# Handing over between two layers in token halves

## The reference, cut to what matters

```python
def _hybrid_layer(x, ..., w_out, g_post):
    ...
    o = jnp.concatenate([o_mla, o_fox], axis=-1) @ w_out
    return x + _rms_norm(o, g_post)

def second_block(x, w_in, ..., norm_g, final_g):
    ...
        h = _rmsnorm(x, norm_g[l])
        proj = h @ w_in[l]
        (qa, kca, vca, ksa, vsa, kwa, vwa, za, ga,
         qb, kb, vb, zb) = jnp.split(proj, offsets, axis=-1)
```

## Time and profile before

| | |
|---|---|
| median of 3 runs | 1853.12 us (1852.43 to 1853.68) |
| the profiled execution | 1853.12 us |
| its span | 1851.4 us |
| mean granted TensorE clock | 0.994 |
| PE busy | 1823.4 us (98%) |
| DVE busy | 1047.4 us (57%) |
| ACT busy | 665.6 us (36%) |
| POOL busy | 36.3 us (2%) |

### The profile page before, as it was taken

One profiled execution on the slowest core, in us unless ns is written; L12 is line 12 of the kernel. 1 busy time (PEld: TensorE's weight loads), 2 busy tenths in 40 slices (PEclk: granted clock), 3 DMA queues, 4 the chain that ended last, 5 costly groups with the idle time before them and its releaser, 6 DMA issues.

```text
span 1851.4 us, 25537 instructions
## 1 busy us (share of the span) xinstructions
PE 1823.4 (98%) x9060; PEld 1514.8 (82%) x9060; DVE 1047.4 (57%) x1768; ACT 665.6 (36%) x1279; POOL 36.3 (2%) x58
## 2 busy tenths in 40 slices
PE   9999999999999999999999999999999999999997
PEld 7788888888888887878868887888888888888887
DVE  7643434444433787853348954766767566665334
ACT  6532332322223544432226342433433333443222
POOL 0000000000000000000002000000000000000001
PEclk9999999999999999999999999999999999999998
DMA  6322222222232333232237363211112222124333
GB/s 237 106 86 91 79 79 91 86 84 82 89 102 80 126 114 113 91 112 93 91 101 218 102 227 124 70 57 57 68 57 69 92 68 79 66 70 136 115 115 102
DMA packets 56021, 186.16 MB, mean 101 GB/s; under 512 B 6688, under 2 KB 11168, under 8 KB 55456
## 3 DMA queue, kind: packets, MB, share of 16 engines
q1 hardware_dynamic: 51328, 170.78, 27.6%
q0 software_dynamic: 4640, 14.68, 3.0%
HBM read 177.05 MB, written 8.39 MB: 100 GB/s over the span
## 4 chain that ended last, share of the span: by engine, by line
PE 90%; DVE 5%; DVEq 2%; ACT 1%; issue 1%; POOL 0%; POOLq 0%; ACTq 0%
PE strip L421 23%; PE strip L423 22%; PE strip L422 22%; PE scores L421 4%; PE scores L422 3%; PE scores L423 3%; PE outputs L423 2%; PE outputs L422 2%; PE outputs L421 1%; PE scores L476 1%; PE scores L869 1%; PE scores L828 1%; PE scores L897 1%; DVE wl L1433 1%; DVEq L1438 0%
## 5 line engine op out<-in xcount | busy, mean ns | idle before, releaser
L421 PE MATMUL strip<-xh,wh 128*128 128x512 f32 (+1 forms) x1976 | 779.7, 395 | 5.7 <-DVE xl L1825 3.2
L423 PE MATMUL strip<-xh,wl 128*128 128x512 f32 (+1 forms) x1976 | 768.0, 389 | 0.0
L422 PE MATMUL strip<-xl,wh 128*128 128x512 f32 (+1 forms) x1976 | 767.2, 388 | 0.0
L421 PEld LDWEIGHTS strip<-xh,wh 128*128 128x128 f32 x1976 | 371.9, 188 | 82.4 <-DVE xl L1825 4.8
L423 PEld LDWEIGHTS strip<-xh,wl 128*128 128x128 f32 x1976 | 371.6, 188 | 77.3
L422 PEld LDWEIGHTS strip<-xl,wh 128*128 128x128 f32 x1976 | 372.3, 188 | 72.7 <-issue 0.7
L1433 DVE TENSOR_TENSOR wl<-raw,wh 128x1024 fp32r<-128x1024 f32 (+3 forms) x306 | 354.7, 1177 | 119.1 <-ACT wh L979 118.2
L979 ACT ACTIVATE wh<-raw 128x1024 fp32r<-128x1024 f32 (+3 forms) x308 | 306.9, 1023 | 109.7 <-PE strip L423 107.1
L1001 ACT ACTIVATE prob<-scores,nms 128x128 f32<-128x128 f32 (+3 forms) x128 | 65.9, 532 | 129.7 <-DVE nms L1481 129.7
L1241 ACT ACTIVATE e_t<-o 128x512 f32 (+1 forms) x30 | 19.0, 632 | 222.0 <-DVE o L1902 118.1
L421 PE MATMUL scores<-xh,wh 128*128 128x512 f32 (+1 forms) x240 | 91.6, 382 | 0.0
(11 more groups left out here) (426 smaller groups left out, 1875.6 us busy)
## 6 DMA issues: line engine op xcount, KB each, us to landing
raw<-in_w SPq DMA_DIRECT2D x308, 512.0 KB, 3.2
xn<-o POOLq DMA_DIRECT2D x4, 1024.0 KB, 7.8
xr<-xn POOLq DMA_DIRECT2D x16, 256.0 KB, 3.0
o<-in_xt SPq DMA_DIRECT2D x7, 512.0 KB, 7.9
o<-in_xt POOLq DMA_DIRECT2D x14, 256.0 KB, 6.3
out<-o SPq DMA_DIRECT2D x14, 256.0 KB, 2.7
raw<-in_w SPq DMA_DIRECT2D x2, 256.0 KB, 4.6
o<-in_xt SPq DMA_DIRECT2D x2, 256.0 KB, 5.1
```

The lines of the kernel that those rows point to most:

```text
L421: pe.matmul(out, ah, bh, start=first, stop=False, skip_group_check=shared)
L422: pe.matmul(out, ah, bl, start=False, stop=False, skip_group_check=shared)
L423: return pe.matmul(out, al, bh, start=False, stop=last, skip_group_check=shared)
```

## The change

The last two strips of w_out (14 and 15) are made for tokens 0 to 255 of both, then for tokens 256 to 511 (`pe_half_strip`). The sums of the first half stand after five steps of the third of these four half strips, its spread after that half strip. The six filler matmuls are gone. `pe_mid` takes the place of `pe_four`: it goes over the first six tiles (`HT`) for the first half of the tokens, then over the same for the second half, then over tiles 6 to 15 whole. The sums of the second half stand after tile 1 of the first pass, its spread (all 512 columns, into `px`) after tile 3. VectorE scales, adds residuals and takes rests of the first six tiles in halves, the accumulating DMAs of tiles 2 to 5 are halves too (eight for four), and the squares of the six tiles as well. Squares go to a sum of their own, `acc_mid`, which GpSimd clears, through four buffers. Other parts only have their counts of semaphores shifted.

```diff
-WARM_FIRST, WARM_MID = 5, 6
+WARM_FIRST = 5
+HT = 6
...
+        g.memset(acc_mid[:, :], 0.0).then_inc(blk_zero, 1)
...
-        for j in range(2, KT):
-            if j >= 6:
-                x_is_added(j - 4)
-            g.wait_ge(scaled, j - 1)
+        for hf in range(2):
+            for j in range(2, HT):
+                if hf:
+                    g.wait_ge(x_added[j % 4], 16)
+                g.wait_ge(scaled, HT * hf + j + 1)
+                g.dma_start(o[:, j, TOKENS[hf]], d["xt"][:, j, TOKENS[hf]], accum_op=ALU.add).then_inc(x_added[j % 4], 16)
+        for j in range(HT, KT):
+            g.wait_ge(x_added[j % 4], 16 * (2 + (j - HT) // 4))
+            g.wait_ge(scaled, HT + j + 1)
             g.dma_start(o[:, j, :], d["xt"][:, j, :], accum_op=ALU.add).then_inc(x_added[j % 4], 16)
...
+    def pe_mid(pe, u0, outs, aside):
...
+        for hf in range(2):
+            for j in range(HT):
+                pe.wait_ge(x_lo, X_MID + HT * hf + j + 1)
+                if hf == 0 and j % 2 == 0:
+                    pe.wait_ge(w_lo, u0 + j // 2 + 1)
+                for s in range(4):
+                    ins = tile(j, s, TOKENS[hf], hf == 0 and j == 0, False)
+                if hf == 1 and j % 2 == 1:
+                    ins.then_inc(w_used, 1)
+                if hf == 0:
+                    aside(j)
+        for u in range(HT // 2, 8):
+            if u == 7:
+                pe.wait_ge(sq_used, KT + HT + KT)
+                pe.matmul(px[:, :], ones[:, :], acc_mid[:, :], start=True, stop=True).then_inc(sum_done, 1)
...
-        pe_token_sums(pe, 3, N_OUT1 + KT)
-        pe_spread(pe, 0, (po,))
-        for i in range(WARM_MID):
-            pe.matmul(px[:, :], ones[:, :], gate[:, :], start=True, stop=True)
-        pe_four(pe, U_CMPIN, 3 * KT - 6, sb, summed=(4, 7))
...
+        out1_half(0, 0, range(KT))
+        out1_half(0, 1, range(KT))
+        out1_half(1, 0, range(5))
+        pe_half_sums(pe, 0, 4, (half_sq, 2))
+        out1_half(1, 0, range(5, KT))
+        pe.wait_ge(diag_done, 2)
+        pe.matmul(po[:, 0:256], ones[:, :], gate[:, 0:256], start=True, stop=True).then_inc(spread, 1)
+        out1_half(1, 1, range(KT))
+
+        def aside(j):
+
+            if j == 1:
+                pe_half_sums(pe, 1, 5, (ev_act, N_OUT1 + KT))
+            if j == 3:
+                pe.wait_ge(diag_done, NQ)
+                pe.matmul(px[:, :], ones[:, :], gate[:, :], start=True, stop=True).then_inc(spread, 1)
+
+        pe_mid(pe, U_CMPIN, sb, aside)
```

More of the change, by code:

```diff
@@ L546, in pe_sum, with pe_half_sums @@
         pe.matmul(px[:, :], ones[:, :], squares[:, :], start=True, stop=True).then_inc(sum_done, 1)
-    def pe_token_sums(pe, i, squared):
-        pe.wait_ge(acc_ready, i + 1)
-        for t in range(NQ):
-            pe.matmul(px[:, t:t + 1], acc[:, P * t:P * t + P], ones[:, 0:1], start=t == 0, stop=False,
+    def pe_half_sums(pe, hf, added, squared):
+        pe.wait_ge(acc_ready, added)
+        for t in (2 * hf, 2 * hf + 1):
+            pe.matmul(px[:, t:t + 1], acc[:, P * t:P * t + P], ones[:, 0:1], start=t == 2 * hf, stop=False,
@@ L553, in pe_token_sums, with pe_half_strip @@
                       skip_group_check=True)
-        pe.wait_ge(ev_act, squared)
-        for t in range(NQ):
-            ins = pe.matmul(px[:, t:t + 1], e_t[:, P * t:P * t + P], ones[:, 0:1], start=False, stop=t == NQ - 1,
+        pe.wait_ge(*squared)
+        for t in (2 * hf, 2 * hf + 1):
+            ins = pe.matmul(px[:, t:t + 1], e_t[:, P * t:P * t + P], ones[:, 0:1], start=False, stop=t == 2 * hf + 1,
                             skip_group_check=True)
         ins.then_inc(sum_done, 1)
-    def pe_spread(pe, k_, banks):
-        for out in banks:
-            pe.wait_ge(diag_done, NQ * (k_ + 1))
-            pe.matmul(out[:, :], ones[:, :], gate[:, :], start=True, stop=True).then_inc(spread, 1)
+    def pe_half_strip(pe, u0, out, hf, steps):
+        for k_ in steps:
+            u = u0 + k_ // 8
+            if k_ % 8 == 0:
+                pe.wait_ge(w_lo, u + 1)
+            cols = slice(P * (k_ % 8), P * (k_ % 8) + P)
+            ins = three(pe, out[:, 0:256], wh[u % SLOTS][:, cols], wl[u % SLOTS][:, cols], xh[:, k_, TOKENS[hf]],
+                        xl[:, k_, TOKENS[hf]], k_ == 0, k_ == KT - 1)
+            if hf == 1 and k_ % 8 == 7:
+                ins.then_inc(w_used, 1)
+        if hf == 0 and k_ == KT - 1:
+            ins.then_inc(part_done, 1)
@@ L1249, in _ @@
+        half_square(0, 0)
+        half_square(0, 1)
+        act_root(a, 3, 0, 2)
+        half_square(1, 0)
+        act_hi(a, At(U_CMPIN))
+        xh_half(0, 0)
+        xh_half(0, 1)
+        act_hi(a, At(U_CMPIN + 1))
+        xh_half(0, 2)
+        for j in range(3):
+            sq_half(0, j)
+        xh_half(0, 3)
+        half_square(1, 1)
         act_hi(a, At(U_CMPIN + 2))
+        xh_half(0, 4)
+        sq_half(0, 3)
+        xh_half(0, 5)
+        act_root(a, 4, 2, 4)
         act_hi(a, At(U_CMPIN + 3))
-        act_root(a, 3)
@@ L1253, in _ @@
[L1253 to L1263 removed]
+        for j in (4, 5):
+            sq_half(0, j)
@@ L1932, in _, with residual @@
[L1932 to L1940 removed]
+        for j in range(2):
+            lo(v_, At(U_CMPIN - 2 + j))
+        out1_half(0, 0)
+        half_add(0)
+        out1_half(0, 1)
+        token_rms(v_, 3, 0, 2)
+        def residual(hf, j):
+            v_.drain()
+            part = o[:, j, TOKENS[hf]]
+            v_.tensor_tensor(part, part, xr1[:, j, TOKENS[hf]], ALU.add).then_inc(xn_done, 1)
@@ new lines, in _ @@
+        scale_half(0, 0)
+        scale_half(0, 1)
+        v_.wait_ge(xr1_in, 16)
+        residual(0, 0)
+        half_add(1)
+        v_.drain().then_inc(r_done, 1)
+        scale_half(0, 2)
+        residual(0, 1)
+        scale_half(0, 3)
+        rest_half(0, 0)
+        lo(v_, At(U_CMPIN))
+        rest_half(0, 1)
+        scale_half(0, 4)
+        scale_half(0, 5)
+        lo(v_, At(U_CMPIN + 1))
+        rest_half(0, 2)
+        out1_half(1, 1)
+        v_.drain().then_inc(r_done, 1)
+        v_.wait_ge(blk_zero, 2)
@@ new lines, in _ @@
+        square_half(0, 0)
+        rest_half(0, 3)
+        lo(v_, At(U_CMPIN + 2))
+        square_half(0, 1)
+        token_rms(v_, 4, 2, 4)
+        rest_half(0, 4)
+        rest_half(0, 5)
+        v_.wait_ge(spread, 2)
+        scale_half(1, 0)
+        scale_half(1, 1)
+        residual(1, 0)
+        scale_half(1, 2)
+        residual(1, 1)
+        scale_half(1, 3)
+        rest_half(1, 0)
+        rest_half(1, 1)
+        scale_half(1, 4)
+        scale_half(1, 5)
+        lo(v_, At(U_CMPIN + 3))
@@ L1951, in _ @@
+        for j in range(KT - 2, KT):
+            square_tile(j)
         lo(v_, At(U_CMPIN + 8))
-        rms_ms(v_, 4, D)
-        rms_rb(v_, 4, rb)
+        rms_ms(v_, 5, D)
+        rms_rb(v_, 5, rb)
         v_.wait_ge(tab2_in, 32)
```

235 lines of the change are left out of this document (159 added, 76 removed).

## The result

The changed kernel takes 1857.8 us (median of 12 runs, 1856.1 to 1860.9), the kernel before 1853.1 us beside it (12 runs, 1852.2 to 1855.0). The ratio is 1.0026 with a 95% interval of 1.0018 to 1.0034: it is 4.7 us slower. The forecast was 1853.9 us with a range up to 1858.5, and most of its weight lay on "no difference"; the time is in the range, 0.7 us from its upper end, on the side that had 0.20. One execution of a later kernel (e5) was slow, with 9088.8 us, and is left out of its median.

What follows compares the result with a forecast made beforehand. VectorE's queue was taken to bound the changed kernel: 952.4 + 42.7 + 8.4 + 5.2 puts the last square at 1008.7 against 1007.88, 0.8 us later, so 1853.12 + 0.8 = 1853.9 us, range 1847.5 to 1858.5.

Steps and rivals of the forecast that it cites:

- The bound: Between the layers: TensorE's 14.3 us without products goes, but VectorE, with 3.7 us of slack, decides through its last square.
- TensorE's side: Strips 14 and 15 in halves, sums and first spread: 933.67 to 958.0; product starts 11.8 us earlier.
- VectorE's work: From the first scaling to the last square: 42.7 us as before plus 8.4 us added by the halves.
- VectorE's waits W: VectorE's stalls for ScalarE between first scaling and last square: 4.5 to 5.8 us, taken as 5.2.
- the stepping: Four engines' queues walked in program order with measured durations; it gave the waits, and the old last square within 0.7 us.
- the main case: VectorE's work and waits set the end: 1853.9 us, own range 1850.5 to 1857 (waits 2 to 8.3), chance 0.56.
- the second root: VectorE waits for ScalarE's root of the second half, behind the copy of tile 5: 0.6 to 1.2 us.
- the last tiles and a late residue of weights: VectorE's waits late in the product, for one later residue and the last tile: 0.9 us.
- The clock: TensorE's new waits of 1.5 to 3 us can halve its clock twice: 2.0 us more, 1855.9 us; chance 0.06.
- A half transfer takes as long as a whole: Eight half transfers occupy the DMA engines 1.7 us each: 5.2 us slower, 1858.3 us; chance 0.15.
- VectorE without waits: Halves land before VectorE asks, so its stalls vanish: 4.4 us gained, 1848.7 us; chance 0.15.
- TensorE sets the pace: VectorE does its added work in less, so TensorE's full 9.1 us comes: 1844.0 us; chance 0.08.

Runs made afterwards that it cites:

- e5: Changed kernel with the second half's root ahead of two copies, weight loads held for tile 5's first half, and four 1 MB stores last: 1853.8 us.
- e4: Changed kernel with weight loads from the product's fifth unit on held until tile 5's first half has landed: 1855.1 us.
- e7: Changed kernel with five filler matmuls put into each of TensorE's three long waits: 1858.6 us.
- e8: e5 with five filler matmuls put into each of the same three places on TensorE: 1856.8 us.
- e9: e5 with the twelve half squares added by TensorE instead of VectorE: 1851.0 us.
- e3: Changed kernel with the four 1 MB stores moved behind the last accumulating transfer: 1857.6 us.
- e1: Changed kernel with the second half's root on ScalarE ahead of the copies of tiles 4 and 5: 1855.1 us.

## Why the prediction was right in its frame and short in one term

**The bound: right.** TensorE's hole is gone and the end of the stretch still hangs on VectorE's last square (wait 2.7 us). The 9.1 us that TensorE alone would gain didn't come.

**TensorE's side: right.** Four half strips with their sums and first spread take 934.78 to 959.12, 24.34 us; the forecast had 933.67 to 958.0, 24.33. The waits before tile 6 (2.96 for "about 3") and before the sum are there; the one before the second spread is 3.1 us for 1.5 to 2.

**VectorE's work: right.** From 953.57 to the end of the last squares at 1013.95 are 60.4 us. Its waits in it are 8.85 us, so the work is 51.5; the forecast's 42.7 + 8.4 is 51.1. All the durations and drains together are off by 0.4 us.

**VectorE's waits W: the step that failed.** The stalls were 8.85 us for 5.2, above the upper end of 5.8 that the stepping gave and just past the 8.3 of the main case. By terms: the second root 2.61 for 0.6 to 1.2 (+1.7); the last tiles and a late residue of weights 2.24 + 0.33 for 0.9 (+1.7); the four second-half rests 2.84 (0.57, 0.25, 1.17, 0.85) for some 2.1 (+0.7); the spread 0.43 for 0.4; the first residue 0.40 for 0.85 (−0.45). Sum +3.65 us. But for the 0.33 us of the weight residue, the terms that came out too large all stand behind transfers, and the reason is the landing time: I let every half land after 3.7 us. That holds where nothing else is on the engines (3.1 in the changed kernel, 3.6 in e4), but tiles 4 and 5 went out beside weight loads and took 6.1, and the last whole tiles took 7.6 where I carried 4.4 from the first transfer of the kernel before. The forecast had named landings of "4.4 us and more" as a sign of being wrong. The earlier trace rows had shown the DMA share at 1.02 in just this stage, and the very stretch of the earlier trace rows, 966 to 978, has 5.8 us as the median landing of its seven transfers, the whole program 6.3:

```profile
o<-in_xt POOLq DMA_DIRECT2D x7, 256.0 KB, 5.8
o<-in_xt POOLq DMA_DIRECT2D x14, 256.0 KB, 6.3
```

e4 shows it by taking the load away: with halves landing at 3.6 us, the second root's term goes to 0.3 us and W to 5.2, the forecast's own number, and start to sum to 75.6 for the forecast's 75.0 (1008.7 − 933.67). In part the terms cancel there: the root is 0.6 us below its forecast, the four rests 1.1 above (3.2).

**The clock: right that it falls, small in the median.** It fell to half near 988 and 1015, behind waits of 2.96 and 2.73 us. The first was absorbed by the wait at the sum. The second was not and cost 1.7 us in that execution (8.06 us from sum to strip for 6.34), where the rival had 1.0 for each of two. The filler runs don't show it in the median, where it would have to return. The Trainium skill (TensorE: Matmul & The Clock Gate, section "Part 1: The HAM clock gate") has the gate fall after idleness; the trace agrees at these two places. But idleness of this length doesn't always bring a fall: behind the 3.09 us wait before the second spread, in 969 to 973, the clock stayed at 1.00. Filling all three waits made the medians 0.8 and 2.9 us longer (e7 and e8).

**The sum of the profiled execution.** 1.1 us of late start, 4.1 us on VectorE (60.4 for 56.3), 0.8 that the forecast already had, 1.7 behind the sum: 7.7, and 1860.88 less 1853.12 is 7.8. On the median it is 4.7, of which the forecast had 0.8.

**The rivals.** "A half transfer takes as long as a whole" gave 1858.3, next to the 1857.8 measured, but by another mechanism: it made every half slow for its rows. It needed a service of at least 1.25 us per half; the engines spent 0.90 us on one, by the row above, close to the 0.95 that the forecast took. Undisturbed halves land 1.3 us ahead of a whole one (3.1 for 4.4), and what is slow is whatever shares the engines with weights and stores, half or whole. By the fit of the Trainium skill (DMA: Bandwidth & Descriptors, section "Anatomy of one DMA — SWDGE (gpsimd) path"), set on the measured whole, a half would have landed at 4.1 us; the undisturbed rows are below that, the others 2 us above, so the figure was off to both sides. "VectorE without waits" and "TensorE sets the pace" were wrong for this kernel; e9 (start to sum 70.3 us) comes within 5.2 us of TensorE's pace (998.8 − 933.67 = 65.1), and only with both chains cut; 1.4 us of the 5.2 (12 × 0.12) are the additions that it gave to TensorE.

**The chances.** The main case's own range ended at 1857 and 0.20 stood for "slower"; by the rows at hand, landings of 4.4 to 8 us under load should have had more than the 0.15 that one mechanism got. That the time fell inside the stated range is in part luck: the range reached 1858.5 only for the sake of the slow halves, which is not what happened.

## What to carry to other kernels

Starting a consumer earlier moves its transfers to an earlier place, too: ask what else is on the DMA engines there, and take a landing time measured under that load, not the first one after a quiet stretch. Where an early start exposes two chains of similar length, test the remedies together and not only alone: e4 or the moved additions alone recovered 3.6 and 1.9 us, all of them 8.9. Before two profiles are compared between marks, compare the granted clock between them, too. And a root, or any step that a whole pipeline waits for, doesn't belong behind copies that wait for a transfer.

## What the runs showed of the hardware

- An accumulating transfer of 128 KB landed 3.1 us after its issue with the engines free, 6.1 beside two 512 KB weight loads; one of 256 KB took 4.4 as the first of its stretch, 4.3 (e3) and 7.6 (changed kernel) in 997 to 1004 without and with the 1 MB stores among them.
- A matrix of ones times a square of 256 columns costs TensorE 0.12 us as a rounded operand in one pass, against 0.43 us and a drain for the addition on VectorE. The fillers, of 256 columns too but in full precision, cost 0.46 each. The rows are six of the additions in e9, of which each next starts 0.12 us after the one before, and five fillers in e7, which are ten entries.

```profile
972.30 0.88 PE L610 MATMUL outputs<-sqr,ones_r 128*128 128x256 f32 x6
1011.01 2.32 PE L597 MATMUL outputs<-gate,ones 128*128 128x256 f32 x10
```

- A wait of TensorE of 2 to 3 us was followed in some executions by a fall of the granted clock to half (a mean of 0.6 in the two short stretches above), in others by none: before tile 6 TensorE waited 3.0 us in the changed kernel and in e1 alike, and only the first fell. Far behind the change, in 1128 to 1142, the clock was 1.00 in e1's profile and 0.88 in that of the changed kernel:

```profile
1128.00:1142.00 14.00, 11.78 (x54) 8.26 (x53) 6.18 (x9) 2.91 (x5) 0.00 (x0) 1.00 0.30 99
```

```profile
1128.00:1142.00 14.00, 11.78 (x49) 7.49 (x48) 6.34 (x10) 2.73 (x5) 0.00 (x0) 0.88 0.46 150
```

  From the strip behind the sum to the end it then took 834.8 us in e1 and 837.1 in the changed kernel, 2.3 us that no edit in this study put there. What decides whether the clock falls at a given place stays open; it is why single profiles are compared between two marks here and not by their spans.
